# Last expert's weights loaded in two steps, final norm pipelined over three engines, result rows loaded from two queues

## What is computed

```python
h = h + mixer(rms_norm(h));  h = h + cross_attention(rms_norm(h), mem_k, mem_v)
xn = rms_norm(h)
# router: best of 4 groups, then best 2 of its 8 experts, with weights gate[t, 0..1]
h = h + sum(gate[t, k] * (silu(xn @ w_gate[e]) * (xn @ w_up[e])) @ w_down[e]  for k, e in choices(t))
y = h * rsqrt(mean(h * h) + 1e-6) * norm_final
```

## Time and profile before

| | |
|---|---|
| median of 3 runs | 2323.11 us (2322.73 to 2330.76) |
| the profiled execution | 2317.78 us, span 2316.1 us, granted clock 0.958 |
| PE busy | 2104.0 us (91%) |
| PE weight loads busy | 1186.5 us (51%) |
| DVE busy | 599.5 us (26%) |
| ACT busy | 472.4 us (20%) |
| POOL busy | 258.4 us (11%) |
| HBM traffic | 201 GB/s over the span |

### The profile page before, as it was taken

How to read it: one execution, slowest core, us unless ns; L and a number is a source line. 1 busy time by engine, 2 the same in 40 slices (tenths; PEclk the granted TensorE clock), 3 DMA queues, 4 the chain that set the end, 5 groups by cost and what they waited for, 6 DMA issues and landing times.

```text
span 2316.1 us, 33699 instructions
## 1 busy us (share of the span) xinstructions
PE 2104.0 (91%) x12706; PEld 1186.5 (51%) x12706; DVE 599.5 (26%) x1416; ACT 472.4 (20%) x1013; POOL 258.4 (11%) x402
## 2 busy tenths in 40 slices
PE   6999998999969999999999999898599999999971
PEld 4577765666635665666665446646333333333320
DVE  4221224666610140111111020622511111111116
ACT  3212223444410000000000021403122222212112
POOL 1001222322221000000000000000011111111110
PEclk9999999999979999999999999997799999999995
DMA  8356778887894124002002120400989999999946
GB/s 313 106 156 215 248 268 280 288 263 260 256 335 137 37 82 146 1 1 73 1 0 82 37 87 1 155 1 33 351 300 377 383 375 368 375 373 372 372 186 230
DMA packets 193546, 458.65 MB, mean 198 GB/s; under 512 B 18465, under 2 KB 27698, under 8 KB 193258
## 3 DMA queue, kind: packets, MB, share of 16 engines
q1 hardware_dynamic: 161306, 360.06, 43.9%
q0 software_dynamic: 32080, 96.44, 12.3%
HBM read 432.51 MB, written 32.17 MB: 201 GB/s over the span
## 4 chain that ended last, share of the span: by engine, by line
PE 81%; DMA 7%; DVE 4%; issue 3%; SPq 2%; ACT 2%; DVEq 1%; POOLq 0%; ACTq 0%; POOL 0%
PE ps L886 19%; PE ps L1288 10%; PE ps L895 7%; PE ps L1319 5%; PE ps L1147 5%; PE ps L1299 5%; PE ps L913 5%; PE ps L1013 4%; PE ps L1217 3%; PE ps L1328 2%; DMA kraw<-in_cache_k 2%; PE ps L928 2%; PE ps L1049 2%; PE ps L1024 2%; PE ps L962 2%
## 5 line engine op out<-in xcount | busy, mean ns | idle before, releaser
L886 PE MATMUL ps<-xnT,ring 128*128 128x352 f32 x1536 | 468.4, 462 | 3.5 <-DMA ring<-in_w_in 2.6
L886 PEld LDWEIGHTS ps<-xnT,ring 128*128 128x128 f32 x1536 | 292.3, 191 | 173.2 <-issue 10.2
L1288 PE MATMUL ps<-gu,xgT 128*64 128x512 f32 x1024 | 228.4, 599 | 12.6 <-DMA wd<-in_w_expert_down 11.7
L2307 POOL DMA_DIRECT2D vpage<-in_cache_v x256 | 137.5, 537 | 435.6 <-issue 426.7
L1013 PE MATMUL ps<-consts,kraw 128*128 128x128 f32 x1024 | 141.4, 283 | 29.3 <-DMA kraw<-in_cache_k 18.7
L1013 PEld LDWEIGHTS ps<-consts,kraw 128*128 128x128 f32 x1024 | 115.3, 144 | 62.1 <-issue 30.3
L1288 PEld LDWEIGHTS ps<-gu,xgT 128*64 128x64 f32 x1024 | 71.4, 138 | 144.6 <-issue 141.5
L1840 DVE COPY kt<-ps 128x512 f32<-128x512 f32 x128 | 88.4, 691 | 185.1 <-PE ps L1013 184.4
L1319 PE MATMUL ps<-wd,hidT_a 128*64 128x512 f32 x512 | 118.6, 605 | 18.3 <-ACT hidT_a L1601 12.3
L895 PE MATMUL ps<-ring,mixT 128*128 128x512 f32 (+1 forms) x288 | 124.0, 593 | 1.3 <-DVE mixT L1982 1.3
L1299 PE MATMUL ps<-gu,xgT 128*32 128x512 f32 x1024 | 115.8, 592 | 0.0
(11 more groups left out here) (341 smaller groups left out, 2386.4 us busy)
## 6 DMA issues: line engine op xcount, KB each, us to landing
kraw<-in_cache_k SPq DMA_DIRECT2D x256, 256.0 KB, 3.7
vpage<-in_cache_v POOLq DMA_DIRECT2D x256, 256.0 KB, 4.7
gu<-in_w_expert_gate SPq DMA_DIRECT2D x32, 2048.0 KB, 20.1
gu<-in_w_expert_up SPq DMA_DIRECT2D x32, 2048.0 KB, 24.8
wd<-in_w_expert_down SPq DMA_DIRECT2D x32, 2048.0 KB, 21.2
ring<-in_w_in SPq DMA_DIRECT2D x7, 2048.0 KB, 9.7
yy<-y_d SPq DMA_DIRECT2D x16, 512.0 KB, 11.4
early<-in_w_in SPq DMA_DIRECT2D x6, 1024.0 KB, 10.6
```

The source lines that it names most:

```text
L886: last = nc.tensor.matmul(bank(R.bank(*tag))[:, 0:NC_], slot[:, k, f * P:(f + 1) * P], xnT[:, k, cols_of(n)], start=k == 0, stop=k == KD - 1)
L1288: last = nc.tensor.matmul(bank(0)[h * BA:(h + 1) * BA, :].rearrange("p (x n) -> p x n", x=2), src[:, k, 0:BA], weight[:, k, :, h * DE // 2 ...
L2307: pool.dma_start(vpage[n % VS][:, p, :], t["cache_v"][ds(page, 1)].rearrange("a s d -> (a s) d")).then_inc(v_in[n % VS], 16)
```

## The change

- SP: ahead of the loop only the wait for expert 28's up result stays. In the loop gate and up are issued after `more_free`, and the down weights after a new semaphore `more_down_free`, which ACT raises when expert 29's down result has been made, and POOL at the end of each turn of the loop.
- PE and ACT: the turn and the copy of the gathered rows stand at the head of the loop's body instead of its end, and those of expert 31 no longer stand in the last turn of the written-out loop. POOL's gather for expert 31 counts on `more_xg_in`.
- Loads of the result rows: SP loads the first choice's rows of the eight prompt tiles and both of tile 8, ACT the second choice's rows of the eight prompt tiles.
- Final norm, tile by tile: ACT squares tile i with a sum, takes the root with 1/D as scale and eps as bias, DVE inverts it behind the sums of tile i + 1, ACT multiplies `resid` by it in place, POOL multiplies by the gain in place, SP stores from `resid`. DVE's scaling passes and the buffers are gone.
- POOL waits for the unused gather behind the loop before its first multiply.

```diff
-            R.made(sp, "gb_e", LAST - GUS), R.made(sp, "db", LAST - WDS)
+            R.made(sp, "gb_e", LAST - GUS)
...
                     sp.dma_start(gu[LAST % GUS][:, :, x, :], expert_load(j, which)).then_inc(more_w_in, 16)
+                sp.wait_ge(more_down_free, j)
+                apart(sp)
                 sp.dma_start(wd[LAST % WDS], expert_load(j, "w_expert_down")).then_inc(more_w_in, 16)
...
-                for k in range(2):
+                for k in range(2 if i >= PT else 1):
                     sp.dma_start(yy[i % PT][0:r, k, :], y_d[k * NT + i * P:k * NT + i * P + r, :]).then_inc(x_in[i], 16)
...
-                sp.wait_ge(n_fin.scaled, i + 1)
+                sp.wait_ge(fin_scaled, i + 1)
                 dst = t["y_prompt"][i * P:(i + 1) * P, :] if i < PT else t["y_sample"]
-                sp.dma_start(dst, xf[i % 4][0:rows_of(i), :]).then_inc(y_out[i % 4], 16)
+                sp.dma_start(dst, resid[0:rows_of(i), i, :]).then_inc(y_out, 16)
...
@@ tensor
             with pe.Fori(1, n) as j:
+                pe.wait_ge(more_xg_in, j * 16)
+                apart(pe)
+                turn_rows(xg[LAST % 2]).then_inc(more_pe, 1)
                 pe.wait_ge(more_w_in, j * 48)
...
-                pe.wait_ge(more_xg_in, j * 16)
-                apart(pe)
-                turn_rows(xg[LAST % 2]).then_inc(more_pe, 1)
@@ scalar
                 R.made(act, "db", e)
+                if e == LAST - WDS:
+                    act.sem_inc(more_down_free, 1)
...
-            n_fin.act_stats(act, lambda i: resid[:, i, :], lambda i: act.wait_ge(summed, i + 1))
+            act.wait_ge(more_y_out, last * 32)
+            apart(act)
+            for i in range(PT):
+                act.dma_start(yy[i][:, 1, :], y_d[NT + i * P:NT + (i + 1) * P, :]).then_inc(x_in[i], 16)
+
+            def norm_rows(i):
+                r = rows_of(i)
+                act.wait_ge(fin_ready, i + 1)
+                nc.scalar.activation(resid[0:r, i, :], resid[0:r, i, :], ACT.Copy, scale=ss[0:r, 5, i:i + 1]).then_inc(fin_normed, 1)
+
+            for i in range(TILES):
+                r = rows_of(i)
+                act.wait_ge(summed, i + 1)
+                nc.scalar.activation(junk[0:r, :], resid[0:r, i, :], ACT.Square, accum_out=ss[0:r, 4, i:i + 1])
+                act.drain()
+                nc.scalar.activation(ss[:, 5, i:i + 1], ss[:, 4, i:i + 1], ACT.Sqrt, scale=1.0 / D, bias=epsc).then_inc(fin_root, 1)
+                if i:
+                    norm_rows(i - 1)
+            norm_rows(TILES - 1)
@@ vector
+            def invert_root(i):
+                dve.wait_ge(fin_root, i + 1)
+                nc.vector.reciprocal(ss[:, 5, i:i + 1], ss[:, 5, i:i + 1]).then_inc(fin_ready, 1)
...
                 last.then_inc(summed, 1)
-            n_fin.dve_scale(dve, lambda i: resid[:, i, :], 5, lambda i: dve.wait_ge(y_out[i % 4], 16 * (i // 4 + 1)))
+                if i:
+                    invert_root(i - 1)
+            invert_root(TILES - 1)
@@ gpsimd
             last = pool.value_load(nblk[0:1, 1:2], min_val=1, max_val=MAXX + 1)
-            pool.wait_ge(more_xg_in, last * 16)
+            pool.wait_ge(more_xg_in, last * 16 + 16)
             apart(pool)
+            pool.wait_ge(gain_in, 16 * 5)
+            for i in range(TILES):
+                r = rows_of(i)
+                pool.wait_ge(fin_normed, i + 1)
+                nc.gpsimd.tensor_tensor(resid[0:r, i, :], resid[0:r, i, :], gain[0:r, :], ALU.mult).then_inc(fin_scaled, 1)
```

More of the change, by code:

```diff
@@ L181, in build_program @@
         ones = new("ones", [P, 1])
+        epsc = new("epsc", [P, 1])
         pages = new("pages", [1, DB * PAGES], I32)
@@ L406, in build_program @@
                              "odd_y_ready"))
-        more_w_in, more_list_in, more_xg_in, more_y_out, more_free, more_pe, more_act, more_dve = (
-            sem(n) for n in ("more_w_in", "more_list_in", "more_xg_in", "more_y_out", "more_free", "more_pe", "more_act",
-                             "more_dve"))
+        more_w_in, more_list_in, more_xg_in, more_y_out, more_free, more_down_free, more_pe, more_act, more_dve = (
+            sem(n) for n in ("more_w_in", "more_list_in", "more_xg_in", "more_y_out", "more_free", "more_down_free", "more_pe",
+                             "more_act", "more_dve"))
         summed = sem("summed")
-        y_out = [sem(f"y_out{p}") for p in range(4)]
+        y_out, fin_root, fin_ready, fin_normed, fin_scaled = (
+            sem(n) for n in ("y_out", "fin_root", "fin_ready", "fin_normed", "fin_scaled"))
         R = Results(sem("result_full"), sem("read_by_act"), sem("read_by_dve"))
@@ L642, in build_program @@
         n_mix, n_mem = Norm("nmix", 0, TILES, [(0, 2), (2, 5), (5, TILES)]), Norm("nmem", 1, 2)
-        n_xat, n_ffn, n_fin = Norm("nxat", 2, TILES, bufs=xf), Norm("nffn", 3, TILES, bufs=xf), Norm("nfin", 4, TILES, [(0, PT), (PT, TILES)], xf)
+        n_xat, n_ffn = Norm("nxat", 2, TILES, bufs=xf), Norm("nffn", 3, TILES, bufs=xf)
         ring_xo = ring[0].rearrange("p k n -> p (k n)").rearrange("p (k n) -> p k n", k=KC)
@@ L867, in _ @@
                     sp.wait_ge(summed, i - PT + 1)
-                for k in range(2):
+                for k in range(2 if i >= PT else 1):
                     sp.dma_start(yy[i % PT][0:r, k, :], y_d[k * NT + i * P:k * NT + i * P + r, :]).then_inc(x_in[i], 16)
             for i in range(TILES):
-                sp.wait_ge(n_fin.scaled, i + 1)
+                sp.wait_ge(fin_scaled, i + 1)
                 dst = t["y_prompt"][i * P:(i + 1) * P, :] if i < PT else t["y_sample"]
-                sp.dma_start(dst, xf[i % 4][0:rows_of(i), :]).then_inc(y_out[i % 4], 16)
-            for p in range(4):
-                sp.wait_ge(y_out[p], 16 * (3 if p == 0 else 2))
+                sp.dma_start(dst, resid[0:rows_of(i), i, :]).then_inc(y_out, 16)
+            sp.wait_ge(y_out, 16 * TILES)
         @block.tensor
@@ L1365, in _ @@
                     expert_rows(e + 1)
-                else:
-                    pe.wait_ge(xg_in[LAST % 2], 16 * (LAST // 2 + 1))
-                    R.read(pe, "xt_e", e)
-                    turn_rows(xg[LAST % 2]).then_inc(more_pe, 1)
                 R.read(pe, "ta", e)
@@ L1655, in _ @@
                     expert_rows(e + 1)
[L1656 to L1659, removed]
                 if e >= 2:
@@ L1670, in _ @@
             n = act.value_load(nblk[0:1, 0:1], min_val=2, max_val=MAXX + 2)
+            R.made(act, "gb_e", LAST - 2)
             with act.Fori(1, n) as j:
+                act.wait_ge(more_pe, j * 7 - 6)
+                copy_rows(xgT[LAST % 2]).then_inc(more_act, 1)
                 act.wait_ge(more_pe, j * 7 - 5)
@@ L1686, in _ @@
                 copy_odd_y().then_inc(more_act, 1)
-                act.wait_ge(more_pe, j * 7 + 1)
-                copy_rows(xgT[LAST % 2]).then_inc(more_act, 1)
-            n_fin.act_stats(act, lambda i: resid[:, i, :], lambda i: act.wait_ge(summed, i + 1))
+            act.wait_ge(ya_out[0], 16 * ((LAST + 1) // 2)), act.wait_ge(ya_out[1], 16 * (LAST // 2)), act.wait_ge(yb_out, 16 * LAST)
+            last = act.value_load(nblk[0:1, 1:2], min_val=1, max_val=MAXX + 1)
+            act.wait_ge(more_y_out, last * 32)
[15 more added lines that the diff above has]
+            norm_rows(TILES - 1)
         @block.vector
@@ L1695, in _ @@
             nc.vector.memset(ones, 1.0)
+            nc.vector.memset(epsc, EPS)
             dve.drain()
@@ L2360, in expert_gather @@
                         R.made(pool, "xt_e", LAST - 2)
-                gather(xg[e % 2], lists[0:BLK, 0, e:e + 1]).then_inc(xg_in[e % 2], 16)
+                gather(xg[e % 2], lists[0:BLK, 0, e:e + 1]).then_inc(xg_in[e % 2] if e < LAST else more_xg_in, 16)
             def expert_scatter_b(e):
@@ L2387, in _ @@
             expert_scatter_b(LAST - 1)
-            pool.wait_ge(xg_in[LAST % 2], 16 * (LAST // 2 + 1))
-            pool.wait_ge(more_pe, 1)
             n = pool.value_load(nblk[0:1, 0:1], min_val=2, max_val=MAXX + 2)
@@ L2400, in _ @@
                 pool.sem_inc(more_free, 1)
+                pool.sem_inc(more_down_free, 1)
                 load_lists(j + LAST)
```

## The result

The changed kernel took 2333.06 us (median of 8 runs, 2324.84 to 2334.04), the kernel before 2322.76 in as many runs beside it. The ratio is 1.0037 (95% interval 1.0023 to 1.0051), 5.3 to 11.8 us slower. The prediction was 2320.2 us, 2.9 less than before, with 2329 as its upper bound: wrong in sign and outside its range.

The account below looks back on a forecast made before the run. It took the open end to be bound by waiting for the last expert's weights, then the 45.6 us tail. Weights win 9.3 us, exclusion gives back 6.4: 2.9 less, 2320.2 us; range 2307.5 to 2329.

Parts of the forecast that it names:

- Early weights: Last expert: weights issued earlier, so PE starts expert 31 7.6 us sooner; 9.3 us in sum with the clock's share.
- The clock's 1.7 us: First product of expert 31: less PE idling keeps the clock at full speed, saving 1.7 us.
- Rows from two queues: Loading result rows after the last scatter: splitting issue between SP and ACT is worth nothing.
- Exclusion: Final norm: DVE's sums and POOL's multiplies block each other, giving back 6.4 of 9.3 us; chance 0.43.
- X: Time of one POOL multiply by the gain in the final norm, taken as 2.0 us without a row.
- plus the store 2.4: Program end: the last store takes 2.4 us after POOL's last multiply, and its landing ends the span.
- the slower one: Rival in the tail: exclusion with a slow POOL, passing the old tail at 2.3 us a multiply; chance 0.07.

Follow-up runs that it names:

- a_one_queue: The changed kernel with all 18 loads of result rows issued by SP again; ratio to the kernel before 1.0040 (1.0017 to 1.0063).
- a_pool_after: The changed kernel with POOL waiting for the last sum before its first multiply; ratio to the kernel before 1.0045 (1.0027 to 1.0063).
- b_weights: The kernel before with only the change's handling of the last expert (loads, turn, copy, gather); ratio to the kernel before 0.9964 (0.9944 to 0.9985).

## Why the prediction failed

- **Early weights: right, 2 us short.** Gate and up went out 1.7 us behind SP's last load of the loop, the down load 0.9 us behind M. Expert 31 started 7.1 us sooner (7.6 foretold). The clock's 1.7 us came to 0.2: I took the transposes to keep it up, and it fell 4 us behind the last product all the same. The same product took 8.5 to 10.05 us in the seven profiles with this handling, 8.4 to 9.9 in the four with the old one. 7.3 in place of 9.3.
- **Rows from two queues: right.** Nothing gained; the first tile at T + 5.5, the second at T + 8.5. `a_one_queue` has the same within half a us.
- **Exclusion: right in kind, near in size partly by luck.** DVE's passes stretched to 3.2 us, tile 7 was summed at T + 36.7, the last store landed at T + 50.5, foretold T + 52.0. Two errors of the sum took each other back. X was 2.3, not 2.0, which is 2.7 us more over nine multiplies. And a DVE pass and a multiply together took 3.2 us, not 1.28 + 2.3 = 3.6: by `a_pool_after` that overlap is worth 2.6 us. POOL started at T + 16.8 instead of 15.3, with DVE further on. The rule of the Trainium skill on two SBUF operands (SBUF — State Buffer, Who interferes with whom) agrees with this, except that the lock it calls exclusive leaves 0.4 us of each pair running together; what overlaps in them no run shows. Its two-input estimate (GPSIMD Engine Reference, Elementwise — side-by-side cycle accounting), 2.3 us at the low end, was better than my X.
- **The step that failed: "plus the store 2.4" as the end of the program.** The sum ended with the last store's landing because in the kernel before it did. I followed what each moved instruction waits for, but not what POOL does after its last one. Its drain, 10.03 us, was in the trace before, hidden from 2286 to 2296. Making POOL the last engine puts it in the open: the program ends 8.3 us behind the last landing, and 8.0 us later than with the drain paid under cover. None of the rivals had it; the slower one asked for a slow POOL (X from 2.3 on) and was a different mechanism.
- **The sum of it.** Foretold were 2.9 us less. The weights lack 2.0, the tail up to the last landing gives back 1.5, the drain adds 8.3: 5.9 more, as the profiles from M to the end say (99.1 against 93.2). The 1.5 is no more than the noise of single profiles: tails in which nothing was changed took 44.0 to 45.6 us. The medians differ by 10.3, the ratio's interval is 5.3 to 11.8 us. Whether anything lies above 5.9 isn't settled; the interval doesn't ask for it, and single profiles differ by 12 us in M alone.

## What to carry to other kernels

Before giving an engine the last work of a program, look at what it does after its last instruction today and what hides that; here one explicit drain of POOL, placed where other work covered it, took the cost away, in the kernel before and in the changed one. Two-operand multiplies on POOL beside sums of DVE with two operands in SBUF gained 2.6 us over running them one after the other; with DVE's second operand in PSUM neither was slowed. When a wait for data is taken away, look whether the code moved to make that possible is itself the next wait: here the smaller edit won more, by the profiles.

## What was not expected of the hardware

- POOL's first drain took 10034 ns in all seven profiles in which POOL had nothing else left to do; in the changed kernel it ended 10.06 us behind the last multiply. A second drain took 0.04 us, and behind nine multiplies it ended with the last of them.
- The granted clock fell 4 us after PE's last product despite 0.85 us of transposes in between, and in `b_weights` it stayed low for the first 6 us of the next product (10.05 us, clock 0.70 on average).
- DVE with one operand in PSUM and POOL with two in SBUF don't slow each other: 1.3 us a pass and 2.33 us, side by side.
